# Extra dense products on TensorE in the odd tile of a gated DeltaNet step

## The reference

```python
x = x + 0.5 * swiglu(rmsnorm(x, n_f1), f1_g, f1_u, f1_d)
h = rmsnorm(x, n_mix)
proj = h @ w_in
...
y_b, gdn_buf, gdn_s = gdn_mixer(qkv_pre, a_raw, b_raw, z, ...)   # 8 heads of 128, delta rule with states s
merged = jax.nn.sigmoid(gate_a) * (y_a @ w_a) + jax.nn.sigmoid(gate_b) * (y_b @ w_b)
x = x + merged @ w_o
x = x + 0.5 * swiglu(rmsnorm(x, n_f2), f2_g, f2_u, f2_d)
```

## Time and profile before

| | us |
|---|---|
| median of 3 runs | 3563.65 (3559.21 to 3566.44) |
| profiled execution | 3570.27 |
| its span, first to last instruction | 3568.5 |
| PE busy in the span | 3359.5 (94%) |
| odd tile on PE, first to last product | 2225.41 to 2348.9 |

### The profile page before, as it was taken

How to read it: one execution, slowest core, us unless ns; L and a number is a source line. 1 busy time by engine, 2 the same in 40 slices (tenths; PEclk the granted TensorE clock), 3 DMA queues, 4 the chain that set the end, 5 groups by cost and what they waited for, 6 DMA issues and landing times. The chain is left out here.

```text
span 3568.5 us, 51417 instructions
## 1 busy us (share of the span) xinstructions
PE 3359.5 (94%) x20274; PEld 3261.3 (91%) x20274; DVE 1117.5 (31%) x1696; ACT 1045.6 (29%) x1545; POOL 942.9 (26%) x520
## 2 busy tenths in 40 slices
PE   6999999997999799999999999769997999999997
PEld 6999999996999799999999999749997999999996
DVE  4232223224556322232232222232323232223223
ACT  4111111113333344544355453220123111111112
POOL 3112111214223323333233331301234212211212
PEclk8999999998999899999999999569998999999998
DMA  3111111102232212112121210254412111111101
GB/s 122 48 35 48 46 41 41 47 18 83 68 97 86 79 50 66 56 60 62 56 80 49 66 56 32 58 170 153 149 36 65 42 41 47 43 45 41 44 21 51
DMA packets 274431, 222.74 MB, mean 62 GB/s; under 512 B 12043, under 2 KB 251787, under 8 KB 274289
## 3 DMA queue, kind: packets, MB, share of 16 engines
q1 hardware_dynamic: 273988, 220.56, 20.4%
q10 hardware_dynamic: 324, 0.41, 0.0%
HBM read 170.66 MB, written 50.28 MB: 62 GB/s over the span
## 5 line engine op out<-in xcount | busy, mean ns | idle before, releaser
L163 PE MATMUL ffn_bank<-ffn_h_hi,ffn_w_hi 128*128 128x368 f32 x2112 | 699.5, 331 | 40.9 <-DVE ffn_h_lo L428 33.6
L164 PE MATMUL ffn_bank<-ffn_h_lo,ffn_w_hi 128*128 128x368 f32 x2112 | 700.2, 332 | 0.0
L165 PE MATMUL ffn_bank<-ffn_h_hi,ffn_w_lo 128*128 128x368 f32 x2112 | 698.8, 331 | 0.0
L163 PE MATMUL mix_bank<-mix_h_hi,mix_w_hi 128*128 128x368 f32 x1752 | 638.2, 364 | 22.7 <-DVE mix_h_lo L1030 17.1
L385 POOL TENSOR_TENSOR ffn_w_lo<-ffn_w_raw,ffn_w_hi 128x1024 fp32r<-128x1024 f32 x132 | 315.0, 2395 | 1176.6 <-ACT ffn_w_hi L381 1176.6
L164 PE MATMUL mix_bank<-mix_h_lo,mix_w_hi 128*128 128x368 f32 x1752 | 581.3, 332 | 0.0
L165 PE MATMUL mix_bank<-mix_h_hi,mix_w_lo 128*128 128x368 f32 x1752 | 581.1, 332 | 0.0
L163 PEld LDWEIGHTS ffn_bank<-ffn_h_hi,ffn_w_hi 128*128 128x128 f32 x2112 | 399.2, 189 | 42.1 <-issue 42.1
L746 POOL TENSOR_TENSOR mix_w_lo<-mix_w_raw,mix_w_hi 128x1024 fp32r<-128x1024 f32 x73 | 199.5, 2733 | 775.2 <-ACT mix_w_hi L741 775.2
L165 PEld LDWEIGHTS ffn_bank<-ffn_h_hi,ffn_w_lo 128*128 128x128 f32 x2112 | 398.9, 189 | 0.0
L164 PEld LDWEIGHTS ffn_bank<-ffn_h_lo,ffn_w_hi 128*128 128x128 f32 x2112 | 398.8, 189 | 0.0
(11 more groups left out here) (292 smaller groups left out, 4459.7 us busy)
## 6 DMA issues: line engine op xcount, KB each, us to landing
mix_w_raw<-in_w_in SPq DMA_DIRECT2D x73, 512.0 KB, 6.1
ffn_w_raw<-in_ffn_w_gate SPq DMA_DIRECT2D x44, 512.0 KB, 3.8
ffn_w_raw<-in_ffn_w_up SPq DMA_DIRECT2D x44, 512.0 KB, 3.8
ffn_w_raw<-in_ffn_w_down SPq DMA_DIRECT2D x44, 512.0 KB, 3.5
scratch_qkv<-mix_out SPq DMA_DIRECT2D x24, 552.0 KB, 2.8
scratch_x<-g_x SPq DMA_DIRECT2D x8, 552.0 KB, 7.8
scratch_z<-turn_z_out SPq DMA_DIRECT2D x8, 552.0 KB, 2.8
scratch_sig_a<-turn_gate_out SPq DMA_DIRECT2D x8, 552.0 KB, 2.7
```

The source lines that it names most:

```text
L163: pe.matmul(out, w_hi, x_hi, start=first, stop=False)
L164: pe.matmul(out, w_hi, x_lo, start=False, stop=False)
L165: return pe.matmul(out, w_lo, x_hi, start=False, stop=last)
```

## The change

A helper `warm` waits for the bank of a unit and issues one fp32 product of the constant ones (128 by 128) with 512 columns of the constants `con` into it. Nothing reads the result: the unit's own first product starts the bank anew. It is called in front of each odd-tile step whose unit has a bank of its own (all but the first, `dec` of group 0), in front of each pair of heads in `seg`, and in front of each head's `ds`.

```diff
+            def warm(d, unit):
+
+                at = d.name(unit) if d.name(unit) in O.at else unit
+                O.wait_bank(pe, 0, at)
+                pe.matmul(O.ps(at)[:, :], ones, con[:, 0:512], start=True, stop=True)
+
             def odd_step(d, name, k):
                 U, g = d.units, d.g
+                unit = {"zero": "T0", "turn": "rt"}.get(name, f"{name}{k}" if name in ("Y", "X", "T") else name)
+                if d.name(unit) in O.at and (g or name != "dec"):
+                    warm(d, unit)
                 if name == "dec" and g == 0:
...
                     for hd in range(HG):
                         unit = d.name(("sa", "sb")[hd // 2])
                         if hd % 2 == 0:
-                            U.wait_bank(pe, 0, unit)
+                            warm(d, unit)
...
                 elif name == "ds":
+                    warm(d, f"ds{k}_0")
                     pe.wait_ge(d.nu_seg_ready, k + 1)
```

## The result

The changed kernel is slower: 3572.28 us in the median of 8 runs (3571.30 to 3576.30), against 3565.24 for 8 runs of the kernel before (3559.21 to 3570.98). The medians lie 7.0 us apart; the ratio is 1.0026, 95% interval 1.0017 to 1.0035, so some 9 us (6 to 12). The forecast was +12.8 (3576.4) and the range 3566 to 3598.

A forecast was written before the change was run, and what follows sets the result against it. The prediction took the stage to be bound by PE at half its clock. Its steps A to F summed to +12.8 us, from a median of 3563.65 to 3576.4 us, range 3566 to 3598.

The forecast's parts named there:

- A: Decay and norms, 2221 to 2255 us: dense products before the sums of squares delay ScalarE, +3.5 us (bounds +0.9, +5.1).
- B: Second key products to last level, 2255.2 to 2275.1 us: 22 dense products, own work mostly at 2.4 GHz, +11.1 us.
- C: Segments' products, 2275.1 to 2305.9 us: four dense products at 1.2 GHz, first 4.0 us still at 2.4 GHz, +2.8 us.
- D: Turn and solve, 2305.9 to 2316.0 us: dense products before turns and solves, clock up for the solves, +1.7 us.
- from the solve to the first head: Stretch after the solve: first head product still 3.3 us after it, set by VectorE's work, unchanged.
- E: Head states, 2316.0 to 2346.8 us: clock up, VectorE then limits, 24.2 against 30.8 us, -6.6 us.
- F: Last sums: first takes 0.86 + 0.55 us instead of 1.1, ScalarE's chain and stage end as before, +0.3 us.
- the stage never leaves 2.4 GHz: Rival: segments' products also at 2.4 GHz, C at -12.0; sum -2.0 (3561.7), or -8.3 (3555.3) at other bounds; 6% each.
- the head states stay at 1.2 GHz: Rival: 80-row products don't bring the clock up in the head states, E at +13.6, sum +33.0 us (3596.7); 10%.
- Little changes: Rival: clock up from the sums of squares through a second pair of segments' products, sum +4.0 us (3567.7); 10%.

## Why the prediction was right

The direction and the mechanism held: PE pays for each dense product, the clock comes up where the rows of the kernel before had something like the main loop and not where they had 16-column passes, and the sum of both signs is a small loss. By its steps:

| step | forecast | measured | before and after |
|---|---|---|---|
| A, decay and norms | +3.5 | +3.0 | 29.85 and 32.84 us |
| B, levels | +11.1 | +12.0 | 19.93 and 31.93 |
| C, segments' products | +2.8 | +1.0 | 30.72 and 31.76 |
| D, turn and solve | +1.7 | +1.8 | 6.84 and 8.69 |
| from the solve to the first head | 0 | -0.5 | 3.33 and 2.80 |
| E, head states | -6.6 | -8.0 | 30.80 and 22.79 |
| F, last sums and the rest to the merge | +0.3 | +0.3 | rest of the count |
| sum | +12.8 | +9.6 | 154.6 and 164.2 |

The sum was 3 us too high. Most of that is C and E, with B the other way.

C: I let the clock outlast the dense work by 4.0 us, by the row after the main loop. It outlasted the levels by 6.2 us, with the first two of the four dense products still at 0.59 to 0.68 us a pass. Without the four it was some 2 us, so the row after the main loop did not carry over. My two errors, too long a time and no help from the four, cancel in part, which is luck.

E: I gave VectorE 23.51 us and 0.7 of hand-offs; it had 21.71 us of work in the stretch of 22.79. The masked copies were the same (10.83 us before, 10.71 now). The adding of new states was not (11.07 and 9.46 us): 0.7 us more of it now lies behind the stretch's end, and the three adds of a head, one right behind the other, take 1.34 us where they took 1.44 or more in two or three pieces. The first of the eight dense products is in the row above.

B: I took a dense product at 0.86 us, and among level steps it is 0.90 from its start to the step's, 22 x 0.04 = 0.9 us.

The other 1 us is A and the way to the first head, 0.5 us each. I had the latter as unchanged and set by VectorE, which misread the rows: PE's products for the outputs filled it at 0.50 without a pause (3.33 us, no idle time in the earlier trace rows before the first head). At 1.00 they take 1.90 us, and the dense product behind them 0.90. F fits by its number only, since that part took 31.8 to 35.3 us over the runs.

The price of one product (0.86 and 1.70 us) fits: passes of 0.59 to 0.68 and of 1.06 to 1.22 us, near those of the earlier trace rows. That dense products in front of a wait for their own bank can't use it also holds: PE's long wait is 9.8 us, now in front of the dense product instead of the sum.

```profile
PE mix_a_bank L1381 <- ACT odd_dec L1510: 9.8, 1, 9.8
PE mix_a_bank L1309 <- DVE odd_kq L1664: 3.4, 2, 2.3
```

Of the rivals, "the stage never leaves 2.4 GHz" fails in C at 0.50 for 25.5 us, as the forecast said it would; "the head states stay at 1.2 GHz" fails at 1.00 for 22.8. They would have stayed there without their eight dense products, as that experiment shows (30.8 us at 0.50). "Little changes" fails in A and B (+3.0 and +12.0 instead of +0.9 and +9.6), and in C, where the clock fell early in the second pair.

## What to carry to other kernels

A product that is there only for TensorE's clock is worth its own time where it brings the engine to 2.4 GHz and is small against the work it speeds up; nearly the same clock (0.89 against 0.95) was to be had in the levels for 128 columns instead of 512, and in the segments' products 24 short products held it where 4 and 8 long ones lost it. So size them by stretch, don't put them where they only delay others, and look at the granted clock of each stretch rather than at the sum. An engine without a pause in the profile may still be running at half its clock.

## What was not expected of the hardware

What held the clock did not raise it. With dense products of 80 rows the clock stayed at 0.50 in the decay steps, where those of 128 rows brought it up in five of five kernels; but products of 80 rows, those dense ones among them, then kept 1.00 through the 22.6 us of the head states, at whose start the clock was up.

Near the edge it isn't steady: with 192 columns at every third segment the clock held for 18 us of like work and then fell, and four runs of that kernel lay 17 us apart, of which this fall explains some 7 by the estimate above.
